# The last token tile of a hybrid layer's mixing stage in halves, expert weights requested by halves as their slots are released, and routing without the matrix products that nothing reads

## The reference

```python
mixed = concat(rmsnorm(y_pool), rmsnorm(o_nsa), rmsnorm(o_mem))   # each with its part of g_mix
h  = x + mixed @ w_out                      # 1024 x 1024
hn = rmsnorm(h, g_ffn)
y  = h + hier_moe(hn)

def hier_moe(x):
    l1 = x @ w_router1 + b_router1          # 4 groups
    p1 = softmax(l1); top1_p, grp = top_k(p1, 1)
    l2 = (x @ w_router2 + b_router2)[grp]   # 8 experts of the chosen group
    top_v, top_i = top_k(l2, 2)
    w = softmax(top_v) * top1_p
    # for each of 32 experts e, with combine weight c[:, e]:
    y += (silu(x @ w_gate[e]) * (x @ w_up[e]) * c[:, e]) @ w_down[e]   # 1024 -> 512 -> 1024
```

## Time and profile before

| | us |
|---|---|
| median of three runs | 1099.66 (1095.79 to 1101.13) |
| the profiled execution | 1101.71 |
| its span | 1099.8 |
| TensorE busy in it | 923.7 (84%) |
| VectorE busy | 323.3 (29%) |
| ScalarE busy | 192.8 (18%) |
| POOL busy | 112.7 (10%) |
| mean rate of all DMA | 248 GB/s, 273.11 MB |

### The profile page before, as it was taken

How to read it: one execution, slowest core, us unless ns; L and a number is a source line. 1 busy time by engine, 2 the same in 40 slices (tenths; PEclk the granted TensorE clock), 3 DMA queues, 4 the chain that set the end, 5 groups by cost and what they waited for, 6 DMA issues and landing times. The chain is left out here.

```text
span 1099.8 us, 13550 instructions
## 1 busy us (share of the span) xinstructions
PE 923.7 (84%) x5427; PEld 503.2 (46%) x5427; DVE 323.3 (29%) x694; ACT 192.8 (18%) x462; POOL 112.7 (10%) x131
## 2 busy tenths in 40 slices
PE   4899969998967887889989899987787777777874
PEld 2455535554544553444555455543344333334432
DVE  3333252413343558854433111111111111111110
ACT  1121121202103457551100010000000000000000
POOL 0000114112000000000000021111101101101111
PEclk9899989999977678989987999999999999999998
DMA  9754018476207000005739499999999999999992
GB/s 388 305 185 106 14 57 205 115 178 173 77 2 277 1 1 1 1 1 208 293 145 399 176 388 411 412 414 416 418 415 415 418 410 411 416 413 412 411 389 57
DMA packets 66055, 273.11 MB, mean 248 GB/s; under 512 B 11760, under 2 KB 27951, under 8 KB 40575
## 3 DMA queue, kind: packets, MB, share of 16 engines
q1 hardware_dynamic: 52215, 255.18, 59.5%
q0 software_dynamic: 7376, 12.85, 4.3%
q10 hardware_dynamic: 6400, 4.20, 1.6%
HBM read 265.64 MB, written 19.10 MB: 259 GB/s over the span
## 5 line engine op out<-in xcount | busy, mean ns | idle before, releaser
L2107 PE MATMUL ps<-room 128*64 128x256 f32 x800 | 97.2, 389 | 32.2 <-DMA room<-in_w_up 18.2
L2107 PE MATMUL ps<-w_a,room 128*64 128x256 f32 x576 | 70.0, 391 | 22.1 <-DMA w_a<-in_w_up 12.6
L2107 PEld LDWEIGHTS ps<-room 128*64 128x64 f32 x800 | 56.7, 138 | 69.2 <-DMA room<-in_w_up 27.2
L2107 PE MATMUL ps<-w_b,room 128*64 128x256 f32 x576 | 68.3, 383 | 23.4 <-DMA w_b<-in_w_up 12.9
L441 PE MATMUL ps<-w_b,room 128*128 128x454 f32 (+1 forms) x240 | 81.8, 552 | 0.7 <-ACT room L414 0.7
L2016 POOL DMA_INDIRECT out_y<-room,halves x32 | 50.1, 1565 | 294.8 <-ACT room L2285 291.3
L2285 ACT ACTIVATE room<-ps,slot_w 128x512 f32<-128x512 f32 x32 | 22.0, 687 | 283.5 <-PE ps L2132 283.5
L2107 PEld LDWEIGHTS ps<-w_a,room 128*64 128x64 f32 x576 | 41.0, 139 | 48.4 <-DMA w_a<-in_w_up 18.0
L2107 PEld LDWEIGHTS ps<-w_b,room 128*64 128x64 f32 x576 | 40.2, 137 | 48.8 <-DMA w_b<-in_w_up 18.3
L890 PE MATMUL ps<-room,w_a 128*128 128x378 f32 x192 | 62.0, 482 | 0.0
L2195 DVE SCALAR_TENSOR_TENSOR room<-room,ps 128x256 f32<-128x256 f32 x32 | 13.5, 421 | 161.4 <-ACT room L2279 161.4
(11 more groups left out here) (351 smaller groups left out, 1216.9 us busy)
## 6 DMA issues: line engine op xcount, KB each, us to landing
room<-in_w_down SPq DMA_DIRECT2D x26, 1024.0 KB, 28.6
room<-in_w_gate SPq DMA_DIRECT2D x25, 1024.0 KB, 28.0
room<-in_w_up SPq DMA_DIRECT2D x25, 1024.0 KB, 28.9
w_a<-in_w_gate SPq DMA_DIRECT2D x18, 1024.0 KB, 27.6
w_a<-in_w_up SPq DMA_DIRECT2D x18, 1024.0 KB, 27.8
w_a<-in_w_down SPq DMA_DIRECT2D x18, 1024.0 KB, 29.4
w_b<-in_w_gate SPq DMA_DIRECT2D x18, 1024.0 KB, 28.6
w_b<-in_w_up SPq DMA_DIRECT2D x18, 1024.0 KB, 28.2
```

Of the source, the lines that this page charges most:

```text
L2107: ins = nc.tensor.matmul(ps[h * CAP:h * CAP + CAP, bank, 0:FH], xT[:, n // 2 % 2, k, CAP * slot:CAP * slot + CAP], w[k // 4][:, k % 4, h * ...
```

## The change

**The last position in halves.** `out_proj` of position 4 is split into its two column halves, with the router product of position 2 and the turn of position 3 between them. A new `weigh_last` adds x and multiplies by the gain half by half, and TensorE turns these rows without the factor of the norm. The sum of squares follows; the factor is applied to the 36 logits (`scalar_tensor_tensor` in `logits`), and to the rows that are stored in `scale_last`, once they are turned. ScalarE copies the turned rows of position i - 1 ahead of the root of position i.

**Units.** The x rows of the last position lie in `bands` instead of the part of `spare` that belongs to slot 10, and the rows of positions 0 and 1 at the end of the working area. Unit 10 is requested after position 2's stores, when position 1's are done. In the block `experts` every half of a unit is requested when the products on that half of the slot's last unit are done (`first_half` counts them), and the first 24 requests go in the order in which TensorE uses the slots (`uses`).

**Routing.** `stay_awake` and its five calls are gone, with 15 products.

The diff, cut to its core:

```diff
-        self.rows4 = [self.xin4[:, 0, :], self.xin4[:, 1, :], self.xg[:, 0, :], self.xg[:, 1, :], self.kcv[:, 0:D]]
+        self.rows4 = [self.xin4[:, 0, :], self.xin4[:, 1, :], self.xg[:, 0, :], self.xg[:, 1, :], self.bands[:, 0:D]]
...
-        hcount = [sum(1 if t < TILES else 4 for t in OUT_ORDER[:i + 1]) for i in range(NT)]
+        hcount = [sum(4 if t == TILES else 1 + (t == OUT_ORDER[-1]) for t in OUT_ORDER[:i + 1]) for i in range(NT)]
...
-            between = [(6, 7), (0, 1), (2,), (), ()]
+            between = [(6, 7), (0, 1), (2,), (10,), (3,)]
             for i, t in enumerate(OUT_ORDER):
                 r = ROWS[t]
                 if i == 2:
                     sp.wait_ge(normed, TILES + 1)
+                if i == 3:
+                    sp.wait_ge(stored[1], 32)
                 if i == NT - 1:
                     sp.wait_ge(h_in_psum, hcount[i])
-                    self.load_unit(sp, 3)
                 for u in between[i]:
                     self.load_unit(sp, u)
                 sp.wait_ge(hn_ready, i + 1)
...
             sp.wait_ge(l_in_psum, NT)
             self.load_unit(sp, 8)
-            sp.wait_ge(hn_ready, NT)
-            self.load_unit(sp, 10)
             sp.wait_ge(l_out, NT)
             self.load_unit(sp, 5)
...
             def turn_hn(i):
                 r = ROWS[OUT_ORDER[i]]
-                pe.wait_ge(hn_ready, i + 1)
+                if i < NT - 1:
+                    pe.wait_ge(hn_ready, i + 1)
+                else:
+                    pe.wait_ge(hg_ready, 1)
                 if i >= 1:
                     pe.wait_ge(hT_ready, i)
...
-            def stay_awake(n):
-
-                for _ in range(n):
-                    nc.tensor.matmul(ps[:, 3, :], self.c(C_ONE, P), self.consts[:, 0:512], start=True, stop=True)
-
             out_proj(0)
             last_ssq()
             pe.wait_ge(o_out, TILES)
-            for i in range(1, NT):
+            for i in range(1, NT - 1):
                 out_proj(i)
                 if i >= 2:
                     router(i - 2)
                 turn_hn(i - 1)
+            out_proj(NT - 1, (0,))
+            router(NT - 3)
+            turn_hn(NT - 2)
+            out_proj(NT - 1, (1,))
             router(NT - 2)
-            stay_awake(3)
             turn_hn(NT - 1)
-            stay_awake(1)
             router(NT - 1)
-            stay_awake(6)
             pe.wait_ge(pair_ready, 1)
...
-            stay_awake(1)
             pe.wait_ge(hot_ready, 1)
...
                 ins.then_inc(done, 1)
-            stay_awake(4)
...
                     for a in range(4):
                         ins = nc.scalar.copy(spread[0:r, 256 * a:256 * a + 256], ps[32 * a:32 * a + r, 2 * (i % 2), 0:256])
                     ins.then_inc(h_copied, 1)
+                if i >= 1:
+                    route(i - 1)
                 act.wait_ge(hms, i + 1)
                 nc.scalar.activation(sq[0:r, 1:2], sq[0:r, 0:1], ACT.Sqrt).then_inc(hroot, 1)
-                if i >= 1:
-                    route(i - 1)
             route(NT - 1)
             act.wait_ge(lclear, 1)
...
+            def weigh_last():
+                i, rows = NT - 1, hn[:, (NT - 1) % 2, :]
+                dve.wait_ge(x_in[i], 16)
+                dve.wait_ge(stored[i % 2], 32 * (i // 2))
+                for a in range(2):
+                    half = slice(512 * a, 512 * a + 512)
+                    dve.wait_ge(h_in_psum, hcount[i] - 1 + a)
+                    ch.then(nc.vector.tensor_tensor(h[i][:, half], ps[:, 2 * (i % 2) + a, :], xin[i][:, half], ALU.add))
+                    ins = nc.vector.tensor_tensor(rows[:, half], h[i][:, half], gf[:, half], ALU.mult)
+                ins.then_inc(hg_ready, 1)
+                ch.then(nc.vector.tensor_tensor_reduce(xin[0], h[i], h[i], 1.0, 0.0, ALU.mult, ALU.add, sq[:, 2:3]))
+                nc.vector.tensor_scalar(sq[:, 0:1], sq[:, 2:3], 1.0 / D, EPS, ALU.mult, ALU.add).then_inc(hms, 1)
+            def scale_last():
+                dve.wait_ge(hroot, NT)
+                ch.then(nc.vector.reciprocal(sq[:, 3:4], sq[:, 1:2]))
+                dve.wait_ge(hT_in_psum, NT)
+                rows = hn[:, (NT - 1) % 2, :]
+                nc.vector.tensor_scalar(rows, rows, sq[:, 3:4], None, ALU.mult).then_inc(hn_ready, 1)
             def logits(i):
                 t = OUT_ORDER[i]
                 dve.wait_ge(l_in_psum, i + 1)
+                if i == NT - 1:
+                    nc.vector.scalar_tensor_tensor(lg[:, t, :], ps[:, 6 + i % 2, 0:36], sq[:, 3:4], br, ALU.mult, ALU.add).then_inc(l_out, 1)
+                    return
                 nc.vector.tensor_tensor(lg[0:ROWS[t], t, :], ps[0:ROWS[t], 6 + i % 2, 0:36], br[0:ROWS[t], :], ALU.add).then_inc(l_out, 1)
-            for i in range(NT):
+            for i in range(NT - 1):
                 norm_h(i)
                 if i < 2:
                     late_scales[i]()
                 if i >= 1:
                     logits(i - 1)
+            weigh_last()
+            logits(NT - 2)
+            scale_last()
             logits(NT - 1)
...
-    def load_unit(self, sp, u):
+    def load_unit(self, sp, u, parts=(0, 1)):
         n, m = u // 3, u % 3
         if m < 2:
             src = self.ins[("w_gate", "w_up")[m]].rearrange("(e p k) f -> e p k f", p=P, k=KD)[n]
-            for j in range(2):
+            for j in parts:
                 sp.dma_start(self.gate_or_up(u, j), src[:, 4 * j:4 * j + 4, :]).then_inc(self.unit_in[j][u % RING], 16)
         else:
             src = self.ins["w_down"].rearrange("(e h p j) d -> e p h j d", h=2, p=P, j=KF // 2)[n]
-            for j in range(2):
+            for j in parts:
                 sp.dma_start(self.down_half(u, j), src[:, j, :, :]).then_inc(self.unit_in[j][u % RING], 16)
...
+        uses = [(0, 0), (0, 1)] + [(n + d, m) for n in range(NEXP) for d, m in ((1, 0), (1, 1), (0, 2)) if n + d < NEXP]
+        place = {3 * n + m: i for i, (n, m) in enumerate(uses)}
...
         @block.sync
         def _(sp):
-            for u in range(RING, NU):
-                if u >= RING:
-                    n, m = (u - RING) // 3, (u - RING) % 3
-                    if m == 0:
-                        sp.wait_ge(gate_done, 2 * n + 2)
-                    elif m == 1:
-                        sp.wait_ge(up_done, 2 * n + 2)
-                    else:
-                        sp.wait_ge(y_in_psum, 2 * n + 2)
-                self.load_unit(sp, u)
+            again = [3 * n + m + RING for n, m in uses[:24]]
+            again += [u for u in range(RING, NU) if u not in again]
+            for u in again:
+                n, m = (u - RING) // 3, (u - RING) % 3
+                sp.wait_ge(first_half, place[u - RING] + 1)
+                self.load_unit(sp, u, (0,))
+                sp.wait_ge((gate_done, up_done, y_in_psum)[m], 2 * n + 2)
+                self.load_unit(sp, u, (1,))
...
                                                    start=(k == 0), stop=(k == KD - 1))
                             if k == KD - 1:
                                 ins.then_inc(done, 1)
+                        if k == KD // 2 - 1:
+                            ins.then_inc(first_half, 1)
...
                                                start=(k == 0), stop=(k == KF - 1))
                         if k == KF - 1:
                             ins.then_inc(y_in_psum, 1)
+                    if k == KF // 2 - 1:
+                        ins.then_inc(first_half, 1)
```

More of the change, by code:

```diff
@@ L1058, in alloc_mix @@
         w, ROW = self.w_b, D + 256 + 36
-        (area, mT, mz, mkT, xin, rms, state, w_pool, cols, w_router, gate, stt, sq, _) = self.front_parts(
-            (4 * D, KD * NTOK, 1024, 512, 2 * D, 256, 256, 128, 10, KD * 36, TILES * 24, 6 * 32, 8, 434))
+        (area, mT, mz, mkT, rms, state, w_pool, cols, w_router, gate, stt, sq, xin) = self.front_parts(
+            (4 * D, KD * NTOK, 1024, 512, 256, 256, 128, 10, KD * 36, TILES * 24, 6 * 32, 8, 2 * D))
         self.area, self.late_room = area, mT
@@ L1646, in mix @@
         sq = self.sq
-        hcount = [sum(1 if t < TILES else 4 for t in OUT_ORDER[:i + 1]) for i in range(NT)]
+        hcount = [sum(4 if t == TILES else 1 + (t == OUT_ORDER[-1]) for t in OUT_ORDER[:i + 1]) for i in range(NT)]
         stored = [S(f"h_stored{j}") for j in range(2)]
         names = ("mix_dve", "cleared", "h_in_psum", "hms", "hroot", "hn_ready", "hT_in_psum", "hT_ready", "l_in_psum",
-                 "l_out", "lclear", "lexp", "pair_ready", "cnt_in_psum", "tot_in_psum", "h_read", "h_copied", "hot_ready", "hot_w_ready", "table_in_psum", "w_table_in_psum", "table_ready")
+                 "l_out", "lclear", "lexp", "hg_ready", "pair_ready", "cnt_in_psum", "tot_in_psum", "h_read", "h_copied", "hot_ready", "hot_w_ready", "table_in_psum", "w_table_in_psum", "table_ready")
         (steps, cleared, h_in_psum, hms, hroot, hn_ready, hT_in_psum, hT_ready, l_in_psum,
```

(15 more changed lines are left out.)

## The result

The changed kernel takes 1091.03 us (median of 6 runs, 1088.93 to 1094.33) against 1100.39 for the kernel before (6 runs, 1095.79 to 1102.44); the ratio is 0.9923, 95% interval 0.9895 to 0.9951. Measured again later beside other kernels it was 1089.42 against 1099.79, ratio 0.9907 (0.9871 to 0.9943). Both intervals exclude no change, so it is 8 to 10 us faster, where 17 were forecast: the sign was right, the size about half.

A forecast was written before the change was run, and what follows sets the result against it. The prediction took the stream of expert weights as the bound. 12.0 us (earlier first request) plus 5.0 (request order) made 17.0; from 1101.71 that gives 1084.7, and 1083 for the median of runs, range 1077 to 1095.

The forecast's parts named there:

- step 7: First weight request of the expert stage, after half a gate product: 604.6 instead of 616.59, 12.0 us earlier.
- step 8: Start of the expert stage, requests in order of release: 5.0 us more saved, bounds 3 and 6.
- signs of being wrong: First expert after 605, TensorE waiting on neither gather nor POOL; several 13.7 us gate products; under 410 GB/s after 640.
- Steps 1 to 5: Last projection through logits, top experts and tables to the first gather: 592.3 instead of 599.66, bounds 590.3 and 593.7.
- Step 6: Block's end into first expert: gather lands median 5.9 us after issue, at 598.2; first gate product 601.2 instead of 611.16.
- Step 9: Unit 10's earlier request, 5.1 us of weights in the 86 GB/s stretch: nothing alone, the queue only runs dry earlier.
- The rule against the change: Idle TensorE gaps lower the clock, so dropping fillers lengthens what follows; taken up as a gain of 12.9, 1087.
- The late gather with the lower clock: Gather waits out queued weights and first expert runs at low clock: gain 9.1, 1090.6; chance 0.28 for either or both.
- the rival of the lost lead: Block's end waits for something fillers hid, say both gathers' landing; first expert at 608 or later, 1095 to 1097; chance 0.10.

The follow-up runs named there:

- halves_alone: The kernel before with the new request loop (halves, in order of release) and the moved buffers only: 1091.57 us, ratio 0.9927.
- no_last_fillers: The kernel before without its last four fillers, nothing else: 1102.33 us against 1101.83, ratio 1.0011.
- unit10_late: The changed kernel with only unit 10's early request undone (requested last but one, as before): 1091.12 us, ratio 0.9927.
- routing_alone: The changed kernel without unit 10's early request and without the new request loop: 1097.74 us against 1099.08 for the kernel before, ratio 0.9978.

## Why the prediction came out half right

The sum had two terms, 12.0 us by step 7 and 5.0 by step 8. From the start of the last projection, the first request moved by 63.53 - 57.91 = 5.6, and request to end by 5.2. That is 10.8 in the profiles; the other 1.4 of their 12.2 lie ahead of the projection, inside the 5.8 by which its start moves anyway. Beside halves_alone the rest of the change moved the first request by 1.6 only (59.54 to 57.91), though its gather starts 8.5 us earlier. Of the signs of being wrong, one came: the first expert began after 605 (605.86), and what TensorE had waited for was the barrier.

- *Steps 1 to 5* were right, and a little low: from the start of the projection the gather moved by 8.4 where 7.4 were forecast. The prefix count took 2.3 us (581.15 to 583.41, against 2.5) and the totals 2.46 (2.8) at the lower clock, and the tables began 34.1 us from that start (585.80), where 35.1 were forecast.
- *Step 6 failed.* It took 5.9 us from the first gather to the first turn, from a median of landings; measured are 12.2. Two things were wrong in it. The 5.9 is no constant: with weights queued beside them all or nearly all the way, the gathers take 8.0 to 9.9 us, with the queue running dry 5.2 to 6.9, with nothing 3.4 to 3.6. An earlier gather met a fuller queue. The trace of the kernel before had this price: of the seven landings under the median of the earlier trace rows, the four ahead of 636 us took 3.3 to 6.9 us beside a queue that was dry or running dry, the three behind it 8.2 to 8.3. And the block's end waits for the landing of the second gather, started 1.45 us behind the first, with 1.2 us of barrier after it. With these prices the turn comes, by an estimate, at 592.3 + 1.45 + 8.3 + 1.2 = 603.2 instead of 598.2, 5.0 of the 6.3 us that were missed. In the earlier trace rows I took TensorE for the last engine because its fillers ended at 606.09; the second gather, started at 601.11, lands at 607.0 with its 5.9 us, and no_last_fillers shows that it set the turn there.
- *Step 7* was 1.1 too low. The first two turns take 1.09 and 1.12 us at the lower clock, so the expert begins 3.77 after the turn (2.96), and half the gate product takes 3.73 (3.4). Steps 5 to 7 together: -1.0 + 6.3 + 1.1 = 6.4 of the 12.0 lost.
- *Step 8* was right: 5.2 against 5.0, in two pairs: halves_alone and before, and unit10_late and routing_alone, which differ in the request loop alone (477.9 against 483.0).
- *Step 9* was right that the move brings nothing alone; unit10_late lies at 58.08 against 57.91.
- *The rule against the change* was to be weighed more. In the changed kernel the granted clock falls to 0.50, the 1.2 GHz level, at 576 (windows below), after TensorE waited 1.32 us ahead of the last router product and then stood idle from 575.06 on. It is still 0.50 behind the idle 11.38 us, and rises near 610, within the first expert's gate product. The Trainium skill ("TensorE: Matmul & The Clock Gate", section "Why this matters for your kernels") warns of just such gaps, and here the trace agrees. It costs 2.5 us between turn and request against halves_alone (7.50 and 4.95), whose first expert ran at the full rate; against the forecast, which had the first expert cold as in the kernel before, it costs the 1.1 of step 7. The gather's lead over halves_alone, 4.2 us at the turn, more than pays for it.
- *The rivals.* The late gather with the lower clock (1090.6) was closest, with its place right and its mechanism half right: the gathers do not wait the weights out, they share with them. The Trainium skill ("DMA: Bandwidth & Descriptors", section "Queues, rings and completion order") has each DMA engine take turns between the queues, and the trace of unit10_late agrees (8.0 and 9.7 us, both landed ahead of the last weights). That its number lies so near is luck: it had 3.8 us for the late gather and 4.1 for the clock, where 6.3 and 1.1 were lost. That the block's end waits for POOL's landings stood in the rival of the lost lead, where I gave it too little chance.

What POOL does at the end of the block to know of the landings was not seen; only that the release follows a landing by 0.1 us.

Windows of the changed kernel for the clock (the last number but two of a row), from the last router product to the first expert:

```profile
572.00:574.00 2.00, 0.92 (x9) 0.92 (x9) 0.92 (x2) 1.98 (x3) 0.00 (x0) 1.00 1.03 430
574.00:576.00 2.00, 1.06 (x10) 0.94 (x9) 0.79 (x4) 0.33 (x1) 0.00 (x0) 0.93 1.02 375
576.00:580.00 4.00, 0.00 (x0) 0.00 (x0) 3.46 (x16) 0.00 (x0) 0.00 (x0) 0.50 1.01 388
600.00:606.00 6.00, 2.34 (x10) 1.57 (x12) 1.38 (x2) 0.00 (x0) 0.14 (x1) 0.50 0.01 4
606.00:610.00 4.00, 4.00 (x20) 2.25 (x22) 0.00 (x0) 0.00 (x0) 0.86 (x1) 0.52 0.22 64
610.00:614.00 4.00, 4.00 (x40) 2.61 (x38) 0.42 (x1) 0.38 (x1) 0.00 (x0) 1.00 0.84 295
```

## What to carry to other kernels

A chain that ends in a transfer has to be priced with the transfer's time in the traffic that it will meet, not in the one that it met: moved earlier, it can meet a fuller queue and give back nearly half of the lead (8.4 us at the gather, 4.7 at the first turn here). A median over gathers that met a dry queue and gathers that met a full one is the price of neither. Before an engine is named as the last at a barrier, compare every engine, and every transfer that was started ahead of it. Requests sent in the order in which their slots come free, and as soon as half of a slot is free, were worth most of this change: halves_alone has 7.5 us in the medians, the whole 9.4.

## What was not expected of the hardware

From the start of the last projection to the first gather, the eleven profiles of kernels with the changed routing agree within 0.03 us (38.16 to 38.19), while the start itself moves by 5.8 us from one execution to the next. A semaphore that POOL raises behind two indirect DMAs can be seen by SP before the second DMA's own row starts (591.97 against 593.02).
